# Split weights of a two-block transformer in five lent slots around the second block's mixers

## The reference, cut to what matters

```python
x = x + 0.5 * swiglu_ffn_2(rms_norm(x, ffn1_norm[l]), ffn1_w_gate[l], ffn1_w_up[l], ffn1_w_down[l])
h = rms_norm(x, mix_norm[l])
u = h @ w_in[l]                                  # conv 512, pool 256, q 512, k 512, v 512
y_conv = conformer_conv(u_conv, ...)             # 31 taps along the rows, layer norm, silu
y_pool = multiscale_pool(u_pool, pool_w[l], pool_scale[l])
o = diff_attention(q, k, v, lam, slopes)         # 4 heads, two softmax maps each, subtracted
y = jnp.concatenate([y_conv, y_pool, y_attn], axis=-1) @ w_out[l]
x = x + y
x = x + 0.5 * swiglu_ffn_2(rms_norm(x, ffn2_norm[l]), ffn2_w_gate[l], ffn2_w_up[l], ffn2_w_down[l])
x = rms_norm(x, post_norm[l])
```

## Time and profile before

| what | value |
|---|---|
| median of 3 runs | 2064.91 us (2062.87 to 2065.75) |
| the profiled execution | 2065.13 us |
| its span, first to last instruction | 2063.3 us |
| mean granted TensorE clock | 0.998 |
| PE / DVE / ACT / POOL busy | 99% / 73% / 53% / 6% |
| DMA | 378.82 MB, mean 184 GB/s |

### The profile page before, as it was taken

One profiled execution on the slowest core, in us unless ns is written; L12 is line 12 of the kernel. 1 busy time (PEld: TensorE's weight loads), 2 busy tenths in 40 slices (PEclk: granted clock), 3 DMA queues, 4 the chain that ended last, 5 costly groups with the idle time before them and its releaser, 6 DMA issues.

```text
span 2063.3 us, 27840 instructions
## 1 busy us (share of the span) xinstructions
PE 2042.8 (99%) x10800; PEld 1744.7 (85%) x10800; DVE 1499.9 (73%) x2261; ACT 1095.1 (53%) x1637; POOL 128.0 (6%) x140
## 2 busy tenths in 40 slices
PE   9999999999999999999999999999999999999998
PEld 7888888888888888888888888878888888878887
DVE  6776677777677767677767776897677777798766
ACT  5444665544554456655446444675445544675443
POOL 1000100000000001000001000150000000160000
PEclk9999999999999999999999999999999999999999
DMA  7654545555555555455555655436555655435553
GB/s 250 204 184 162 197 153 198 185 184 190 192 185 185 194 165 173 165 194 189 189 192 189 235 193 191 168 115 195 194 191 184 204 185 193 169 107 195 193 193 124
DMA packets 105539, 378.82 MB, mean 184 GB/s; under 512 B 12173, under 2 KB 12837, under 8 KB 105152
## 3 DMA queue, kind: packets, MB, share of 16 engines
q1 hardware_dynamic: 102768, 368.95, 54.1%
q0 software_dynamic: 2208, 7.71, 1.3%
q10 hardware_dynamic: 432, 0.39, 0.1%
HBM read 375.73 MB, written 1.27 MB: 183 GB/s over the span
## 4 chain that ended last, share of the span: by engine, by line
PE 94%; DVE 4%; ACT 1%; DMA 1%; issue 0%; POOL 0%; POOLq 0%; DVEq 0%; ACTq 0%
PE pb L432 31%; PE pb L437 16%; PE pb L360 13%; PE pb L361 13%; PE pb L362 13%; DVE scr L1719 2%; PE pb L385 1%; PE pb L483 1%; PE pb L407 1%; PE pb L406 1%; PE pb L405 1%; DVE wlo L1705 1%; DVE scr L2384 0%; DMA raw<-in_W 0%; PE pb L908 0%
## 5 line engine op out<-in xcount | busy, mean ns | idle before, releaser
L1705 DVE TENSOR_TENSOR wlo<-raw,whi 128x1024 fp32r<-128x1024 f32 (+1 forms) x702 | 847.9, 1215 | 53.7 <-ACT whi L1085 53.2
L1085 ACT ACTIVATE whi<-raw 128x1024 fp32r<-128x1024 f32 (+1 forms) x706 | 730.6, 1045 | 289.1 <-PE pb L437 169.8
L432 PE MATMUL pb<-XT,whi 128*128 128x512 f32 x2816 | 703.1, 391 | 1.8 <-DVE XT L1719 1.3
L432 PEld LDWEIGHTS pb<-XT,whi 128*128 128x128 f32 x2816 | 515.5, 188 | 101.8 <-issue 1.8
L437 PEld LDWEIGHTS pb<-XT,wlo 128*128 128x128 f32 x2816 | 384.1, 190 | 27.5
L437 PE MATMUL pb<-XT,wlo 128*128 128x256 f32 x2816 | 392.6, 282 | 0.0
L1817 DVE TENSOR_REDUCE sbuf_s<-pb 128x256 f32<-128x512 f32 x240 | 154.4, 685 | 235.1 <-PE pb L437 235.1
L360 PE MATMUL pb<-whi,HTh 128*128 128x512 f32 x816 | 321.6, 394 | 0.0
L361 PE MATMUL pb<-wlo,HTh 128*128 128x512 f32 x816 | 319.6, 392 | 0.0
L362 PE MATMUL pb<-whi,HTl 128*128 128x512 f32 x816 | 317.7, 389 | 0.0
L1155 ACT ACTIVATE sbuf_s<-sbuf_s 128x256 f32<-128x256 f32 x120 | 49.7, 419 | 343.1 <-DVE sbuf_s L1824 343.0
(11 more groups left out here) (231 smaller groups left out, 1483.0 us busy)
## 6 DMA issues: line engine op xcount, KB each, us to landing
raw<-in_W SPq DMA_DIRECT2D x694, 512.0 KB, 4.2
raw<-in_W SPq DMA_DIRECT2D x8, 264.0 KB, 2.9
scr<-in_bc POOLq DMA_DIRECT2D x2, 640.0 KB, 5.8
raw<-in_W SPq DMA_DIRECT2D x4, 256.0 KB, 4.7
scr<-scratch POOLq DMA_DIRECT2D x8, 128.0 KB, 4.8
scr<-mrow POOLq DMA_DIRECT2D x2, 512.0 KB, 5.1
scr<-in_slope POOLq DMA_DIRECT2D x1, 1024.0 KB, 11.0
scr<-in_Pg POOLq DMA_DIRECT2D x1, 1024.0 KB, 14.2
```

What stands on the lines that cost most here:

```text
L432: pe.matmul(pb[b + j][:, :], h[:, k:k + P], xs, start=c == 0, stop=False)
L1085: return act.activation(o, i, ACT.Copy, scale=scale)
L1705: dve.tensor_tensor(wlo[u % W_SLOTS][:, 0:c], raw[u % RAW_SLOTS][:, 0:c], whi[u % W_SLOTS][:, 0:c].bitcast(F32), ALU.subtract).then_inc(*u ...
```

## The change

The scratch memory of `mixer2` is ordered anew, so that the attention maps (`pr`, `aT`) lie together. While that memory and the hidden activations `HTh`/`HTl` hold nothing live, they are used as further slots for split weights. Each entry of `lent` has a name, a first and a last unit, and the unit whose use has to be over before the first split. `placed_units` gives every unit of the program a slot: of the free ones the one whose last unit is the oldest. Away from the mixers this is the old cycle of five. For the units around a mixer it gives, worked out from the code:

```diff
+        lent = []
+        for kind, layer, n, m, u0 in stages:
+            if kind == "mixer2":
+                lent += [("aT", u0 - 14, u0 + 17, None), ("pr0", u0 - 10, u0 + 13, None), ("pr1", u0 - 6, u0 + 13, None),
+                         ("H0", u0 + 11, u0 + 13, u0 - 3), ("H1", u0 + 12, u0 + 17, u0 - 1)]
+        def placed_units():
+
+            free = {j: (-1, None) for j in range(W_SLOTS)}
+            places, followed = [], []
+            for u in range(n_units):
+                for name, first_u, last_u, behind in lent:
+                    if u == first_u:
+                        free[name] = (-1, behind)
+                    if u == last_u + 1:
+                        del free[name]
+                slot = min(free, key=lambda j: (free[j][0], str(j)))
+                before, behind = free[slot]
+                places.append(slot)
+                followed.append(before if before >= 0 else behind)
+                free[slot] = (u, None)
+            return places, followed
+        def lead(s, k):
+
+            if s + 1 < len(stages) and stages[s + 1][0] == "mixer2":
+                return AHEAD + (k >= 48) + (k >= 51) + (k >= 54)
+            return AHEAD
...
-                if u >= W_SLOTS:
-                    w.wait_ge(*at("used", u - W_SLOTS))
+                if followed[u] is not None:
+                    w.wait_ge(*at("used", followed[u]))
...
                 square_x(n, 0)
-                split(u0 + 0 + AHEAD)
+                split(u0 + 6)
                 high_x(n, 4)
                 high_x(n, 6)
                 high_x(n, 5)
-                split(u0 + 2 + AHEAD)
+                split(u0 + 8)
                 high_x(n, 7)
-                split(u0 + 1 + AHEAD)
+                split(u0 + 7)
                 square_x(n, 1)
-                split(u0 + 3 + AHEAD)
-                split(u0 + 4 + AHEAD)
+                split(u0 + 9)
+                split(u0 + 10)
+                split(u0 + 11)
+                split(u0 + 12)
                 z_gate(0)
                 z_gate(1)
...
                 turned("q", qT2, gq, 0, 5)
-                split(u0 + 14 + AHEAD)
+                split(u0 + 18)
                 tap(17)
                 turned("q", qT2, gq, 1, 6)
-                split(u0 + 13 + AHEAD)
+                split(u0 + 17)
                 up_high(0)
                 up_high(1)
-                split(u0 + 15 + AHEAD)
                 tap(18)
```

More of the change, by code:

```diff
@@ L189, in program @@
                         ("acc", 512), ("y", 2048), ("q", 1024), ("k", 1024), ("v", 1024), ("qT", 1024), ("kT", 1024),
-                        ("pr", 4096), ("aT", 2048), ("yc", 512), ("tap", 2048)])
+                        ("yc", 512), ("tap", 2048)])
+        c3, n3 = spans([("pr", 4096), ("aT", 2048)])
         bc1, _ = spans(BC1)
@@ L198, in program @@
         scr2 = sb("scr2", [P, n2])
+        ahead = ExitStack()
+        ahead_w = [ahead.enter_context(nc.sbuf_tensor(f"ahead{i}", [P, UC], F32R)) for i in range(6)]
+        ahead.close()
+        scr3 = sb("scr3", [P, n3])
         Pg = sb("Pg", [P, 4, 2, S], F32R)
@@ L287, in program, with lent_slot, high_w, low_w @@
         assert at_unit == n_units
+        lent = []
[3 more added lines that the diff above has]
+                         ("H0", u0 + 11, u0 + 13, u0 - 3), ("H1", u0 + 12, u0 + 17, u0 - 1)]
+        def lent_slot(name):
+            if name in ("pr0", "pr1", "aT"):
+                j = 2 * ("pr0", "pr1", "aT").index(name)
+                return ahead_w[j], ahead_w[j + 1]
+            c = slice(0, 4) if name == "H0" else slice(4, 8)
+            return tuple(a[:, c, :].rearrange("p c t -> p (c t)") for a in (HTh, HTl))
+        def placed_units():
[13 more added lines that the diff above has]
+            return places, followed
+        places, followed = placed_units()
+        def high_w(u):
+            return (whi[places[u]] if isinstance(places[u], int) else lent_slot(places[u])[0])
+        def low_w(u):
+            return (wlo[places[u]] if isinstance(places[u], int) else lent_slot(places[u])[1])
+        def lead(s, k):
+            if s + 1 < len(stages) and stages[s + 1][0] == "mixer2":
+                return AHEAD + (k >= 48) + (k >= 51) + (k >= 54)
+            return AHEAD
+        def split_at(s, k):
+            u = stages[s][4] + k
+            return range(u + (lead(s, k - 1) if k else AHEAD), u + lead(s, k) + 1)
         def layer_of(n):
@@ L1101, in split_half, with step @@
                 copy(whi[u][:, cut], raw[u][:, cut]).then_inc(*(up("hi", u) if half else up("hi", u, "a")))
-            def step(u):
-                split(u + AHEAD)
+            def step(s, k):
+                for u in split_at(s, k):
+                    split(u)
             def high_x(n, c):
@@ L1584, in mixer2 @@
                 tap(11)
-                split(u0 + 9 + AHEAD)
+                split(u0 + 15)
                 tap(14)
-                split(u0 + 11 + AHEAD)
-                split(u0 + 10 + AHEAD)
+                split(u0 + 16)
                 tap(13)
@@ L1639, in mixer2 @@
                 turned_maps(0, 0, 5)
-                split(u0 + 19 + AHEAD)
-                split(u0 + 16 + AHEAD)
-                split(u0 + 17 + AHEAD)
+                split(u0 + 22)
+                split(u0 + 19)
+                split(u0 + 20)
                 value_squares(0, 7)
@@ L2504, in mixer2 @@
                 lam_sum()
-                split(u0 + 5 + AHEAD)
+                split(u0 + 13)
                 tap(0)
@@ L2518, in mixer2 @@
                 tap(11)
-                split(u0 + 7 + AHEAD)
+                split(u0 + 14)
                 head_sum("q")
@@ L2559, in mixer2 @@
                 tap(23)
-                split(u0 + 14 + AHEAD)
+                split(u0 + 18)
                 tap(24)
-                split(u0 + 12 + AHEAD)
                 tap(25)
@@ L2615, in mixer2 @@
                 y_mean(1)
-                split(u0 + 18 + AHEAD)
+                split(u0 + 21)
                 y_root(1)
@@ L2619, in mixer2 @@
                 low_y(0, 6)
-                split(u0 + 20 + AHEAD)
+                split(u0 + 23)
                 low_y(1, 7)
[L2622 to L2626, removed]
+                split(u0 + 24)
+                split(u0 + 26)
+                split(u0 + 25)
+                split(u0 + 27)
+                split(u0 + 28)
                 into_x(u0 + 25, [1.0, 1.0], m)
```

49 lines of the change are left out of this document (22 added, 27 removed).

## The result

The changed kernel took 2073.30 us (median of 5 runs, 2072.33 to 2074.71) against 2064.91 us before (5 runs, 2062.87 to 2066.70). The ratio is 1.0044 (95% interval 1.0033 to 1.0054): slower by 0.44%. The profiled execution took 2073.62 us, its span is 2071.8 us, 8.5 us more than before. The sign, both new waits and the places of both were as forecast; the size was not. The range ended at 2073.0.

A forecast was written before the change was run, and what follows sets the result against it. PE, busy 2042.8 of 2063.3 us, was taken as the bound. First mixer +2.1 and second +0.4 us made +2.5, one clock fall +1.7, together +4.2 us: forecast 2069.1 us, range 2061.5 to 2073 us.

The forecast's parts named there:

- both new waits: PE in each mixer: waits at `turn_z`, +2.8 us, and at `pooled(0)`, +1.0 us in the first mixer, +1.5 in the second.
- The waits taken away: Gaps before `turn_maps` go, -1.70 and -2.26 us, and with the second the fall of the clock, -1.66 us.
- The three earlier splits: Feed-forward stage: 3.7 us of DVE and 3.2 us of ACT, covered by idle time, at no cost.
- The term of `turn_z`, +2.8 us for each mixer: PE waits 1325.15 to 1327.95 for `z_out`, behind late loads of units 11 and 12; bounds 0.1 and 3.4 us.
- the third split comes 0.6 us earlier, by ACT's lost wait: DVE's third split, ahead of loads 11 and 12, comes 0.6 us earlier, so load 12 lands at 1323.8.
- The upper bound of 3.4: `turn_z` in each mixer: the wait is 3.4 us if the third split comes no earlier.
- The term of `pooled(0)`: Split 18 waits for unit 13 ahead of `up_high`: PE gap about 1.9 us, +1.0 us first mixer, +1.5 second.
- Of the four new gaps I count one that costs 1.66 us: One fall of the clock among the new `turn_z` and `pooled(0)` gaps; none and three are the bounds.
- The price: A fall of PE's clock from 2.4 to 1.2 GHz costs 1.66 us.
- Three falls were my own bound: Rival of two or more falls of the clock: 2070.7 us, with three 2072.4; chance 0.21.
- Staying waits: Waits of `logits(1, 0)` and `pool_groups`, chains through DVE's `biased` with no split in them, stay; 2.6 us in all.

The follow-up runs named there:

- DVE's work put back: Against the kernel with both edits: DVE does its halves of splits 17 and 18 twice in each mixer; 2064.31 us, 0.9996 of the kernel before.
- split 18 later: Against the changed kernel: ACT's split 18 moved behind `up_high`, split 17 in its old place; 2069.93 us, 1.0024 of the kernel before.
- fifth raw slot: Against the changed kernel: `RAW_SLOTS` 5 instead of 4, order of splits unchanged; 2067.44 us, 1.0011 of the kernel before.
- 11, 12 later: Against the changed kernel: splits 11 and 12 moved behind `z_gate` on ACT and behind `z_out` and `lam_sum` on DVE; 2063.16 us.
- both edits: Against the changed kernel: splits 11 and 12 behind `z_gate` and `z_out`, and ACT's split 18 behind `up_high`; 2059.57 us, 0.9974 of the kernel before.
- lent slots, old order: Against the changed kernel: lent slots and layout kept, order of all splits and lead of three units as before the change; 2065.26 us.
- both, `job(14, 1)` earlier: Against the kernel with both edits: `job(14, 1)` moved on PE from behind `logits(1, 2)` to ahead of `logits(1, 0)`; 2058.97 us.
- the same, fifth raw slot: Both edits, `job(14, 1)` moved ahead of `logits(1, 0)`, and `RAW_SLOTS` 5 instead of 4; 2058.60 us, 0.9973 of the kernel before.

## Why the prediction was wrong

**The waits taken away** were right in place. The gaps before `turn_maps` went in both mixers, with the fall behind the second. The kernel with DVE's work put back shows DVE's work to be the cause of the gain; at `turn_maps` itself 1.03 us of a gap came back, in one mixer of two. The three earlier splits in the feed-forward stage and the lent memory cost nothing, as said.

**The term of `turn_z`, +2.8 us for each mixer,** measured 3.3 and 3.6 us. What failed is the step "the third split comes 0.6 us earlier, by ACT's lost wait". That wait isn't lost, since unit 8 follows unit 0 in its slot. The table of the change says so. The upper bound of 3.4 was right for the gap alone (3.01 and 3.39). The mechanism, late loads of units 11 and 12, makes about half; the order's own work behind the wait for unit 2 makes the other half, and had no place in my sum.

**The term of `pooled(0)`** was right: a gap of 1.94 us for 1.9, ACT idle for 4.10 for some 4, and split 18's place shown by moving it.

**The clock is the step that failed.** "Of the four new gaps I count one that costs 1.66 us" met three falls, two of them at the logits, behind gaps of 1.9 us that I had thought the safer ones. The price was right (3.66 instead of 2.00 us for the sixteen logits), though PE's path was later by only 1.4 us for each, since a wait of 0.2 us ahead of the logits went. In the profiled executions the change is 8.5 us instead of 4.2. Of these 4.3 us more, the falls are 2.5 (three of 1.4 for one of 1.7), the `turn_z` terms 1.3 and the start of the first mixer 1.4; 0.9 came back at waits that shrank. So the falls are the largest term that was wrong and not the only one. Three falls were my own bound, at 2072.4. What put the time outside the range is that the bound for the number of falls was taken with the middle, and not with the upper end, of the `turn_z` term; 3.4 instead of 2.8, twice, gives 2073.6. The median lies only 0.3 us outside, so the scatter at the start, which was in no term, would do as much.

**Staying waits** were wrong in the other direction. Before `logits(1, 0)` and `pool_groups` 0.80 and 0.82 us became 0.27 and 0.43 in the first mixer. While PE ran the logits at half the clock, DVE caught up. With split 18 later, where the clock did not fall there, the two waits stayed at 1.0 and 1.6 us in all, against 0.5 and 0.9 with the two falls. So some of each fall there was given back, which kept the result from being worse.

Falls in the profiled executions, mixer by mixer, are set against the gaps ahead:

| kernel | gap at `turn_z`, us | fall there | gap at `pooled(0)`, us | fall at the logits |
|---|---|---|---|---|
| changed | 3.01, 3.39 | no, yes | 1.94, 1.93 | yes, yes |
| split 18 later | 3.26, 3.20 | yes, yes | none | no, no |
| fifth raw slot | 1.59, 1.65 | no, no | 1.9 | yes, yes |
| 11, 12 later | none | no, no | 1.9 | yes, no |
| both | none | no, no | none | yes, no |
| lent slots, old order | none | no, no | none | no, yes |
| both, DVE work put back | none | no, no | none | no, yes |
| both, `job(14, 1)` earlier | none | no, no | none | no, no |
| the same, fifth raw slot | none | no, no | none | no, no |

A gap's length doesn't decide it. 3.01 us passed, and with both edits the clock fell with no gap over 0.75 us ahead, in a stretch of narrow matmuls. Filling that stretch's gaps with six wide ones went with no fall in four mixers of two kernels. What decides whether one comes in a given execution stays open.

Each row is one execution, and the number of falls differs between executions of one kernel: the profiled ones have a mean granted clock of 0.997 with two or three falls, 0.998 with one and 0.999 to 1.000 with none, and the five of the changed kernel have 0.996 to 0.998, the quickest (2072.33 us) with the highest. The same figures price the fall of the kernel before: beside the last four kernels its 15 executions at 0.998 took 2065.0 us on average and its three at 1.000 took 2063.25, which is 1.7 us, as the rows had it. With both edits the fall costs nothing that shows: one execution at 1.000 took 2059.71 us, three at 0.998 took 2059.57 to 2059.69. And with `job(14, 1)` earlier all 20 executions of the two kernels have 0.999 or more.

## What to carry to other kernels

More slots for a prepared operand allow an earlier start only as far as the stage ahead has slots too: here four raw slots and in-order loads held the splits that the lent memory let come forward. In an in-order queue, look at each preloading step for what it waits for and what stands behind it: of the mixer's 23 splits, three in the wrong place cost 13.7 us, and without them the change was worth 5.3. Put bounds on the number of the clock's falls together with the upper ends of the waits, not with their middle; here both ran to the upper end at once.

## What the runs showed of the hardware

TensorE fell from 2.4 to 1.2 GHz on waits that look harmless. Sixteen logits took 3.66 us instead of 2.00 after a gap of 1.94 us, and with both edits eight took 2.08 us instead of 1.13 behind gaps of 0.57 and 0.75 us. A fall cost up to 1.66 us, and less where DVE used the time to catch up. The Trainium skill (TensorE: Matmul & The Clock Gate, section "HAM oscillation — how this bites in real kernels") warns of gaps longer than any in the mixers here; the falls in the rows above came without one.

DVE and ACT wrote lent memory next to the mixer's scratch at their usual rate: 1220 and 1049 ns a split, in the kernel with the old order.
